# Other start addresses for the weight rings and the residual stream of a fused two-block transformer kernel

## What is computed

```
h = h + gla_mixer(rmsnorm(h, norm_mix[0]), ...);  h = h + swiglu(rmsnorm(h, norm_ffn[0]), ffn_w_in[0], ffn_w_out[0])
h = h + dsa_mixer(rmsnorm(h, norm_mix[1]), ...);  h = h + swiglu(rmsnorm(h, norm_ffn[1]), ffn_w_in[1], ffn_w_out[1])
x = rmsnorm(h, norm_final)[:, N_META:]
h = h + recurrent_block(rmsnorm_2(h, a_norm), ...);        h = h + sqrelu_mlp(rmsnorm_2(h, mlp_norm[0]), w_up[0], w_down[0])
h = h + chunk_band_attention(q, k, v, ...) @ b_w_o;        h = h + sqrelu_mlp(rmsnorm_2(h, mlp_norm[1]), w_up[1], w_down[1])
```

## Time and profile before

| | us |
|---|---|
| median of 3 runs | 1193.24 |
| lowest, highest | 1191.61, 1193.44 |
| the profiled execution, whole | 1189.84 |
| its span, first to last instruction | 1187.9 |
| TensorE matmuls busy | 1170.2 |
| TensorE weight loads busy | 1135.6 |
| VectorE busy | 826.0 |
| ScalarE busy | 692.4 |
| GpSimd busy | 107.2 |

### The profile page before, as it was taken

The page is one execution under the profiler, slowest core; times in us unless marked ns, Lnnn a source line. Parts: engine busy times, 40 slices in busy tenths (PEclk is TensorE's granted clock), DMA queues, the critical chain, the costliest instruction groups (busy, mean ns, idle before and its releaser), DMA issues. The chain is left out here.

```text
span 1187.9 us, 25975 instructions
## 1 busy us (share of the span) xinstructions
PE 1170.2 (99%) x9722; PEld 1135.6 (96%) x9722; DVE 826.0 (70%) x1287; ACT 692.4 (58%) x1115; POOL 107.2 (9%) x121
## 2 busy tenths in 40 slices
PE   8999999999999899999999999999999999999998
PEld 8998999999998789999999899999999879999998
DVE  7767866666568977766668897675567677766543
ACT  6635765654445567566556986664447476666432
POOL 1000200000100220000120120000013133000000
PEclk9999999999999999999999999999999999999999
DMA  8532655556664336666664565666666424666663
GB/s 274 171 108 84 189 178 175 177 176 197 191 210 131 107 95 190 193 190 188 208 213 148 182 203 181 191 195 194 200 214 208 128 86 145 192 192 189 206 193 107
DMA packets 57578, 207.84 MB, mean 175 GB/s; under 512 B 6353, under 2 KB 7569, under 8 KB 57249
## 3 DMA queue, kind: packets, MB, share of 16 engines
q1 hardware_dynamic: 57136, 203.52, 55.2%
q0 software_dynamic: 288, 3.21, 0.7%
q10 hardware_dynamic: 80, 0.07, 0.0%
HBM read 205.66 MB, written 1.05 MB: 174 GB/s over the span
## 5 line engine op out<-in xcount | busy, mean ns | idle before, releaser
L1676 DVE TENSOR_TENSOR w_lo<-w_raw,w_hi 128x1024 fp32r<-128x1024 f32 x379 | 468.3, 1238 | 69.6 <-ACT w_hi L532 68.9
L532 ACT CAST w_hi<-w_raw 128x1024 fp32r<-128x1024 f32 x379 | 395.3, 1045 | 177.4 <-PE acc L1028 172.9
L1026 PE MATMUL acc<-x_hi,w_hi 128*128 128x256 f32 (+1 forms) x1688 | 478.5, 283 | 3.7 <-DVE w_lo L1676 3.1
L1027 PE MATMUL acc<-x_lo,w_hi 128*128 128x256 f32 (+1 forms) x1688 | 473.1, 280 | 0.0
L1028 PE MATMUL acc<-x_hi,w_lo 128*128 128x256 f32 (+1 forms) x1688 | 472.9, 280 | 0.0
L1026 PEld LDWEIGHTS acc<-x_hi,w_hi 128*128 128x128 f32 x1688 | 317.5, 188 | 8.7 <-issue 4.4
L1027 PEld LDWEIGHTS acc<-x_lo,w_hi 128*128 128x128 f32 x1688 | 317.5, 188 | 0.4
L1028 PEld LDWEIGHTS acc<-x_hi,w_lo 128*128 128x128 f32 x1688 | 317.4, 188 | 0.0
L1026 PE MATMUL acc<-m_hi,w_hi 128*128 128x256 f32 x512 | 141.3, 276 | 0.0
L1027 PE MATMUL acc<-m_lo,w_hi 128*128 128x256 f32 x512 | 141.3, 276 | 0.0
L1028 PE MATMUL acc<-m_hi,w_lo 128*128 128x256 f32 x512 | 141.3, 276 | 0.0
(11 more groups left out here) (359 smaller groups left out, 1683.0 us busy)
## 6 DMA issues: line engine op xcount, KB each, us to landing
w_raw<-weights SPq DMA_DIRECT2D x381, 512.0 KB, 4.2
bias<-bias_rows POOLq DMA_DIRECT2D x1, 2048.0 KB, 10.6
h<-hT SPq DMA_DIRECT2D x4, 272.0 KB, 5.0
bias<-bias_rows POOLq DMA_DIRECT2D x1, 1088.0 KB, 6.8
outT<-h SPq DMA_DIRECT2D x4, 256.0 KB, 4.7
con<-constants SPq DMA_DIRECT2D x1, 913.0 KB, 9.0
w_raw<-weights SPq DMA_DIRECT2D x2, 256.0 KB, 3.8
par<-cols SPq DMA_DIRECT2D x1, 84.0 KB, 1.9
```

What stands on the lines that cost most here:

```text
L532: nc.scalar.copy(w_hi[:, slot, :], w_raw[:, slot, :]).then_inc(hi_ready, 1)
L1026: nc.tensor.matmul(out, wh, xh[:, k, tok], start=first and n == 0, stop=False)
L1027: nc.tensor.matmul(out, wh, xl[:, k, tok], start=False, stop=False)
L1676: V.tensor_tensor(w_lo[:, slot, :], w_raw[:, slot, :], w_hi[:, slot, :].bitcast(F32), ALU.subtract)\
```

## The change

The 192 bytes of `x_pad`, which stood between `h` and `x_hi`, are replaced by 192 bytes of `w_pad` ahead of `w_raw`. So `w_raw`, `w_hi`, `w_lo` and `h` start 192 bytes later, 64 bytes past a multiple of 256 in place of 128 (each of the three rings takes 16384 bytes and h 8704, all multiples of 256), and x and all tiles behind it have the addresses that they had. No instruction changes but for its addresses.

```
         HALF = TILES // 2 * P
+        w_pad = sb("w_pad", [P, 48])
         w_raw = sb("w_raw", [P, RING, TILES * P])
         w_hi = sb("w_hi", [P, RING, TILES * P], F32R)
         w_lo = sb("w_lo", [P, RING, TILES * P], F32R)
         h = sb("h", [P, KD, T])
-        x_pad = sb("x_pad", [P, 48])
         x_hi_rows = sb("x_hi", [P, KD * ROW + 64], F32R)
```

## The result

The changed kernel takes 1227.34 us (median of 4 runs, 1225.41 to 1230.02) against 1193.19 before: a ratio of 1.0299, 95% interval 1.0286 to 1.0313. It is slower by 34 us. The forecast was 1188.2; rival C, the collision of both starts, had 1233. Three of the four runs before lie at 1193.1 to 1193.4, while its profiled execution, at full clock over the whole span, took 1189.84; the changed kernel's two executions at full clock took 1225.41 and 1225.90. At equal clock the loss is therefore about 36 us.

The account below looks back on a forecast made before the run. TensorE's spacing from one matmul start to the next was taken to bound the kernel. All terms were 0 except 5.0 us gained on eighth rows of x and dsa projections: 1193.2 - 5.0 = 1188.2 us, range 1183 to 1235.

Parts of the forecast that it names:

- rival C: TensorE matmuls: the two streams collide when both operands start at the same place; +40 us, 1233; chance 0.25.
- What bounds the kernel: TensorE: the time between matmul starts counts, and whatever shortens or lengthens it passes whole to the end.
- Steps 1 and 2: Adds into h, and splitting and loading weights through the rings: moved starts cost nothing or stay hidden; both taken at 0.
- Step 5: All other matmuls, both operands now at 64: taken at 0, bounds 9 us gained and 45 us lost.
- (64,64): Matmul with moving and stationary operand both starting at 64 modulo 256: claimed as fast as before, 113.3 ns.
- (192,128): Matmul with moving operand at 192 and stationary at 128, eighth rows of dsa: read as slow, about 119.5 to 120 ns.
- Step 4: Eighth rows of x and the dsa projections: weights at 64 speed them up, 5.0 us gained, bounds 0 and 5.4.

Follow-up runs that it names:

- `x_plus32`: Against the kernel before: rings stay at 128 modulo 256, x and all tiles behind it move from 64 to 96; 1217.67 us, ratio 1.0215.
- `x_minus32`: Against the kernel before: rings stay at 128 modulo 256, x and all tiles behind it move from 64 to 32; 1212.08 us, ratio 1.0168.
- `x_plus64`: Against the kernel before: rings and h stay at 128 modulo 256, x and all behind it move from 64 to 128; 1227.11 us, ratio 1.0305.

## Why the prediction was wrong

- What bounds the kernel: right. TensorE's spacing passed to the end, 39.1 us of it, less 3.1 us of waits.
- Steps 1 and 2, h, w_raw, casts, subtractions and DMA at 0: right. h alone gives 0.9994, and the loss is 1.0294 with w_raw left behind, for 1.0299 with it; casts and subtractions keep their lengths in the changed kernel (1043 and 1237 ns for 1045 and 1238).
- Step 5 is the one that failed. It took (64,64) at 0, since "the pair is fast when at least one operand starts at 64". Measured, (64,64) runs at 120.0 ns with 256 columns and at 125.2 to 125.3 in the long stages with 272, and the term came to about 39.5 us. The rule fitted four pairs, but one of the four was misread. The price of (192,128) came from eighth rows of dsa, three matmuls among twenty-one at d = 0, and no row shows what those three cost by themselves. Without that pair the others, (64,128) and (128,64) fast, (128,128) slow, are told apart just as well by the difference, and by that (64,64) is (128,128). Moving everything by 64 bytes separates the two readings.
- Step 4, 5.0 us of relief: the pairs were named rightly, (128,64) in dsa, but priced by the fast one of the two value units shown. The kernel before has eight such units, and by the starts in the timeline the other seven run at 117.8 to 118.0 ns. The dsa projections took this slow rhythm, 117.7 ns, so 288 x 1.8 ns = 0.5 us came in place of 1.8. The eighth rows of x brought nothing, since rows at +64 within a stream at 0 don't get faster: x and m both stand at 120.0.
- Rival C had the place, nearly the price, and the mechanism in part: two equal starts do cost the most at 256 columns, but -32, -96, -128 and +64 are slow too, so it is not a collision of equal starts alone. Its 36 us for 256 columns measured 36. Its 4.3 ns for 272 columns measured 1.3 for x, 1.9 for mid and 3.4 for ga, 3.7 us in place of 9; the relief was 0.6 in place of 5, and 3 us of waits gave way. So about +36 at equal clock, +34 between the medians, came in place of +40; that the total was so near is partly luck, since these misses cancel.
- The chance for C was 0.25 because (192,128) seemed to speak against it. The same misreading set the sign of the forecast and the weight of its rival. The range, 1183 to 1235, held the result only because C was kept inside it.
- The Trainium skill gives TensorE two independent read ports ("TensorE: Matmul & The Clock Gate", section "Step-by-step: what each phase is for") and, among the engines, contention at the port pair shared by VectorE and GpSimd alone ("SBUF — State Buffer", section "SBUF: two separate sides"). By these all kernels here would stay at 1193. They run from 1190 to 1227 us with the same instructions, so here the two reads are not independent of where they start.

## What to carry to other kernels

In this kernel, where matmul and weight load are about equally long, the start of the moving operand relative to that of the stationary one, modulo 256 bytes, is worth 3%. In a kernel of this kind, measure it for the very number of columns, and treat the two addresses as one setting, so that whoever moves one tile moves the other with it. A rhythm is a property of the stream: don't read the price of a pair off a few matmuls that stand among others, and don't expect a third of the cost from a third of the loads. To separate a relative cause from an absolute one, move everything by the same amount.

## What was not expected of the hardware

- Spacing of 256-column float32r matmuls, each with its own 128-column load, by d: 113.3 ns at -64, 117.7 at +64, 118.4 at -32, 117.3 to 118.7 at -96, 118.7 at -128, 120.0 at 0. The best is a single point of the six, not the end of a slope. The value units give two more by the starts, eighth rows included: 116.7 to 118.1 ns at +32 (`x_plus32`) and 118.9 to 119.9 at +96 (`x_minus32`). At 272 columns the order is another: 123.3 to 123.9 at -64 and -96, 125.2 at 0, but 125.8 to 126.7 at -32, +64 and -128.
- At d = -64 and +64 there are two steady rhythms, 113.3 and 117.7 ns. Which one follows is settled at a wait or where other matmuls come between; at -64 either can hold for more than a thousand matmuls, and three matmuls at d = 0 ended the slow one in all four cases seen. Other differences can have two as well: `ga` with 272 columns at d = 0 runs at 126.7 ns in the changed kernel and at 125.3 in `x_plus64`.
- Why -64 is good, and by which path the two reads meet, these runs don't show. That the cause lies in TensorE's two reads of SBUF is what the parts and the idle stretch of the writing engines leave; the mechanism inside is not shown.
